# A hybrid decoder step on one Trainium2 core: token shift, decays, rates and key norms computed inside the projection stage instead of in a stage of their own

## The reference

```python
proj = x @ w_in
pr = proj[..., :RWKV_COLS]
shifted = jnp.concatenate([prev, pr[:, :-1]], axis=1)
mixed = pr + prm['tshift_mu'][i] * (shifted - pr)
...
w_log = -jax.nn.softplus(-(w0 + jnp.tanh(wd) @ w_w2)) - 0.5
decay = jnp.exp(-jnp.exp(w_log))
a = jax.nn.sigmoid(a0 + ad @ w_a2)
g = jax.nn.sigmoid(gd) @ w_g2
kk = heads(k * k_k)
kk = kk / jnp.maximum(jnp.linalg.norm(kk, axis=-1, keepdims=True), 1e-12)
k = k * (1.0 + (a - 1.0) * k_a)
y, S = wkv7_scan(r, decay, k, v, -kk, kk * a, S0)
```

## Time and profile before

| | |
|---|---|
| median of 3 runs | 1966.42 us (1962.9 to 1966.55) |
| the profiled execution | 1965.85 us, span 1963.7 us |
| PE / DVE / ACT / POOL busy | 1602.3 / 709.9 / 347.3 / 230.4 us |
| mean granted clock of TensorE | 0.873 of 2.4 GHz |
| transposes of x | 0 to 30 us |
| `project`, products | 30 to 313 us |
| `attend`, `attend_samples` | 313 to 426, 426 to 466 us |
| `shift_mix` | 466 to 574 us |
| `rwkv_sample` | 574 to 619 us |
| `rwkv_chunks`, `rwkv_norm` | 619 to 884, 884 to 960 us |
| `mix_out` and all after it | 960 to 1964 us |

### The profile page before, as it was taken

How to read it: one execution, slowest core, us unless ns; L and a number is a source line. 1 busy time by engine, 2 the same in 40 slices (tenths; PEclk the granted TensorE clock), 3 DMA queues, 4 the chain that set the end, 5 groups by cost and what they waited for, 6 DMA issues and landing times. The chain is left out here.

```text
span 1963.7 us, 29748 instructions
## 1 busy us (share of the span) xinstructions
PE 1602.3 (82%) x11876; PEld 1020.5 (52%) x11877; DVE 709.9 (36%) x1129; ACT 347.3 (18%) x753; POOL 230.4 (12%) x275
## 2 busy tenths in 40 slices
PE   6999996765522999985399949999959949999978
PEld 5666564544212888873145434444439834444433
DVE  1000000744965555546533341111159641111117
ACT  1000001541311322322000001111112201111111
POOL 3000000003002222303000001001040001100121
PEclk7999997885555999997699959999959959999989
DMA  7224201100011000000411267877750268887634
GB/s 230 99 93 121 107 1 33 46 23 5 0 27 23 4 4 4 4 6 5 118 44 33 94 232 272 294 278 275 243 193 1 88 211 282 288 289 240 212 141 168
DMA packets 134252, 237.09 MB, mean 121 GB/s; under 512 B 20434, under 2 KB 94147, under 8 KB 133866
## 3 DMA queue, kind: packets, MB, share of 16 engines
q1 hardware_dynamic: 110642, 150.94, 23.6%
q0 software_dynamic: 16880, 60.46, 8.4%
q10 hardware_dynamic: 6624, 24.12, 3.0%
HBM read 178.82 MB, written 58.21 MB: 121 GB/s over the span
## 5 line engine op out<-in xcount | busy, mean ns | idle before, releaser
L1985 PE MATMUL ex_pb<-ew_w_gate_up,ex_xT 128*128 x736 | 330.1, 602 | 5.9 <-DVE ex_xT L2025 2.3
L222 PE MATMUL pj_pb<-pj_xT,pj_w 128*128 128x344 f32 (+3 forms) x960 | 282.1, 457 | 0.4 <-ACT pj_xT L232 0.4
L222 PEld LDWEIGHTS pj_pb<-pj_xT,pj_w 128*128 128x128 f32 (+1 forms) x960 | 180.8, 188 | 101.2 <-issue 1.7
L1985 PEld LDWEIGHTS ex_pb<-ew_w_gate_up,ex_xT 128*128 128x128 f32 x736 | 137.9, 192 | 165.3 <-issue 164.4
L1968 PE MATMUL ex_pb<-ew_w_down,ex_hiddenT 128*128 x368 | 165.7, 593 | 3.4 <-ACT ex_hiddenT L2050 3.4
L2174 DVE TENSOR_TENSOR ex_hidden<-ex_hidden,ex_pb 128x256 f32<-128x256 f32 x46 | 19.4, 421 | 324.6 <-ACT ex_hidden L2045 324.6
L1968 PEld LDWEIGHTS ex_pb<-ew_w_down,ex_hiddenT 128*128 128x128 f32 x368 | 66.3, 190 | 69.9 <-issue 69.9
L1932 POOL COPY ex_tokens_now<-ex_token_of_slot 128x1 uint32 (+1 forms) x48 | 9.5, 199 | 745.5 <-PE ex_pb L1957 399.7
L1741 PE MATMUL mo_pb<-mo_w,projected 128*128 128x512 f32 (+1 forms) x144 | 65.8, 611 | 21.3 <-DMA mo_w<-in_w_out 21.3
L2169 DVE COPY ex_y_rows<-ex_pb 128x512 f32<-128x512 f32 x46 | 31.8, 692 | 134.5 <-PE ex_pb L1968 134.5
L238 DVE COPY projected<-pj_pb 128x344 f32<-128x344 f32 (+3 forms) x21 | 10.9, 519 | 187.9 <-PE pj_pb L222 187.9
(11 more groups left out here) (422 smaller groups left out, 2429.5 us busy)
## 6 DMA issues: line engine op xcount, KB each, us to landing
ew_w_gate_up<-in_w_ex_gate SPq DMA_DIRECT2D x32, 1024.0 KB
ew_w_gate_up<-in_w_ex_up SPq DMA_DIRECT2D x32, 1024.0 KB
ew_w_down<-in_w_ex_down SPq DMA_DIRECT2D x32, 1024.0 KB
scratch_slots_out<-ex_y_rows ACTq DMA_DIRECT2D x46, 512.0 KB
scratch_slots_out<-pj_zero POOLq DMA_DIRECT2D x4, 4096.0 KB
scratch_x_stored<-x_rows SPq DMA_DIRECT2D x16, 512.0 KB
pj_w<-in_w_in SPq DMA_DIRECT2D x3, 2048.0 KB, 18.6
pj_xt<-in_x_prompt SPq DMA_DIRECT2D x8, 512.0 KB
```

Of the source, the lines that this page charges most:

```text
L222: last = nc.tensor.matmul(pb[0:mrows, 4 + at % 4, 0:tn], w[:, s % NW, k, c0:c0 + mrows], xT[:, k, t0:t0 + tn], start=(k == 0), stop=(k == ...
L1985: last = mm(pb[:, 2 + u, :], xT[:, u, k, :], w[:, k, :], start=(k == 0), stop=(k == KD - 1))
```

## The change

`shift_mix` is gone. Its work is done in `project`, on products while they come:

- The order of the tiles is now 12, 13 (the inputs of decay, rate and gate), then the keys 4 to 7, then 0 to 3, 8 to 11, and 14 to 19 as before. Weight slabs have 256 columns at most, the first one 192.
- `xT` has a column of zeros ahead, and each product covers one token more on the left (348, 348 and 347 columns in place of 352, 344 and 344), so a product holds each token and the one before it. ACT scales the tokens' own part by 1 - mu out of PSUM; DVE adds mu times the token before, out of the same bank. Only tiles 14 to 19 are still copied in turn.
- TensorE gets 36 small products: after each key tile three for the decay and three for the rate, and after the next two tiles the sums of squares for the key norms, six in each. They use the other four banks of PSUM.
- ACT takes them with sigmoid or square root; DVE does the scan after each key tile, and from the eighth tile on the reciprocals and the products for the keys, in turn.
- The decay sums are kept as plain sums of sigmoids, with one zero ahead of each chunk of 64: the same buffer, read one column earlier, gives the sums before a token. The multiplication by -exp(-0.5) is the scale of the exponentials. In `rwkv_chunks` two exponentials for each tile take the place of three, the second over 130 columns a row.
- `attention_out` is gone: the attention's result is written over the q columns of `projected_qkv`.

The diff, cut to its core:

```diff
-def project(nc, io, pr, pq, keep, const):
+def project(nc, io, pr, A, B, U, pq, vec, keep, const):
-    slabs = [(0, 512), (512, 512), (1024, 512), (NR, WL + AL + GL), (NR + WL + AL + GL, 512),
-             (NR + WL + AL + GL + 512, 256)]
+    slabs = [(NR, WL + AL + GL, ((0, WL + AL, 12), (WL + AL, GL, 13)))]
+    slabs += [(HW * j, HW, ((0, P, 2 * j), (P, P, 2 * j + 1))) for j in (2, 3, 0, 1, 4, 5)]
+    slabs += [(QC + HW * j, HW, ((0, P, 14 + 2 * j), (P, P, 15 + 2 * j))) for j in range(3)]
-    cols = [(0, 352), (352, 344), (696, 344)]
+    thirds = [(0, 347, 347, 348), (347, 347, 347, 348), (694, 330, 338, 347)]
+    cuts = [(0, 384), (384, 384), (768, 264)]
+    FIRST_A, FIRST_N = 2, 6
...
+            def small_products(lhs, rhs):
+                nonlocal small
+                for t0, tn in cuts:
+                    if small >= 4:
+                        pe.wait_ge(s_taken, small - 3)
+                    nc.tensor.matmul(pb[:, small % 4, 0:tn], lhs, rhs[:, t0:t0 + tn], start=True, stop=True).then_inc(s_small, 1)
+                    small += 1
...
+                    before = at - 4
+                    if before >= 3 * MIXED:
+                        pe.wait_ge(s_cp[before % 2], (before - 3 * MIXED) // 2 + 1)
+                    elif before >= 0:
+                        pe.wait_ge(s_mix, before + 1)
...
+                t = i - FIRST_A
+                if 0 <= t < 4:
+                    if t == 0:
+                        pe.wait_ge(s_in, 32)
+                        pe.wait_ge(s_lora, 1)
+                    small_products(w2[:, P * t:P * t + P], pr[0:WL, 12, :])
+                    small_products(a2[:, P * t:P * t + P], pr[0:WL + AL, 12, :])
+                if i in (FIRST_N, FIRST_N + 1):
+                    for t in range(2):
+                        key_norms(2 * (i - FIRST_N) + t)
...
+                    act.wait_ge(s_mm, at + 1)
+                    nc.scalar.activation(pr[0:mrows, tile, t0:t0 + n], product(at)[:, 1:1 + n], ACT.Identity,
+                                         scale=omu[0:mrows, tile:tile + 1]).then_inc(s_now, 1)
...
+            def keys(t):
+                k = pr[:, 4 + t, :]
+                link(stt(out=A[:, t, :], in0=k, scalar=nkk[:, t:t + 1], in1=A[:, t, :], op0=ALU.mult, op1=ALU.mult))
+                link(nc.vector.tensor_scalar(tmp[:, :], B[:, t, :], -1.0, vec["k_a"][:, t:t + 1], ALU.add, ALU.mult))
+                link(stt(out=k, in0=tmp[:, :], scalar=1.0, in1=k, op0=ALU.add, op1=ALU.mult))
+                stt(out=B[:, t, :], in0=A[:, t, :], scalar=-1.0, in1=B[:, t, :], op0=ALU.mult, op1=ALU.mult)
...
+                    last = stt(out=out[:, 0:n_prompt], in0=product(at)[:, 0:n_prompt], scalar=mu, in1=out[:, 0:n_prompt],
+                               op0=ALU.mult, op1=ALU.add)
...
+                t, part = divmod(i - FIRST_N - 1, 2)
+                if 0 <= t < 4:
+                    if i == FIRST_N + 2:
+                        dve.wait_ge(s_slots, 16 * n_zeros)
+                    (inverse_norm, keys)[part](t)
...
-def shift_mix(nc, io, pr, mx, cumx, vec, const):
...
 (rwkv_chunks)
-                nc.scalar.activation(inv[:, :, :], pr[:, 8:12, c], ACT.Exp, scale=-1.0).then_inc(q["ex"], 1)
-                nc.scalar.activation(cumx[:, :, c], cumx[:, :, c], ACT.Exp)
+                nc.scalar.activation(inv[:, :, :].rearrange("p t (h s) -> p t h s", h=2), decays(n, 1), ACT.Exp,
+                                     scale=DECAY).then_inc(q["ex"], 1)
-                nc.scalar.activation(pr[:, 8:12, c], pr[:, 8:12, c], ACT.Exp).then_inc(q["ex"], 1)
+                both = U_[:, :, 2 * (CH + 1) * n:2 * (CH + 1) * (n + 1)]
+                nc.scalar.activation(both, both, ACT.Exp, scale=-DECAY).then_inc(q["ex"], 1)
```

More of the change, by code:

```diff
@@ L43 @@
 TC = TT + NS
-PC = TC + 1
-S0C, V0C = T + 1, T + 1 + NS
+PC = TT + 1
+S0C = T + 1
 DA = 512
@@ L64 @@
 CH = 64
+SC0 = (T // CH) * (CH + 1)
+UW = SC0 + NS
+DECAY = math.exp(-0.5)
 TILES = NT + 1
@@ L159, in project @@
         s_mm = m.sem("product")
-        s_ev = [m.sem(f"evacuated{i}") for i in range(2)]
+        s_now = m.sem("own_part")
+        s_mix = m.sem("mixed")
+        s_cp = [m.sem(f"qkv_copied{i}") for i in range(2)]
+        s_lora = m.sem("tanh")
+        s_small = m.sem("small_product")
+        s_taken = m.sem("small_taken")
+        s_sq = m.sem("squares")
+        s_vec = m.sem("vectors")
+        s_chain = m.sem("chain")
         s_z = m.sem("zeroed")
@@ L166, in project, with product @@
         xp = io["x_prompt"][0]
-        n_out = len(tiles) * 3
+        n_zeros = (NBLK + 7) // 8
+        n_keep = 16 * len(keep)
+        def product(at):
+            return pb[0:tiles[at // 3][2], 4 + at % 4, :]
         @block.sync
@@ L194, in _ @@
                     load_slab(0)
-            for s in range(1, len(slabs)):
+            load_slab(1)
+            sp.wait_ge(s_z, 1)
+            sp.dma_start(w2[:, :], io["decay_w2"][0]).then_inc(s_in, 16)
+            sp.dma_start(a2[WL:WL + AL, :], io["iclr_a2"][0]).then_inc(s_in, 16)
+            for s in range(2, len(slabs)):
                 load_slab(s)
@@ L231, in evacuate @@
                 src = pb[:, 2 * par:2 * par + 2, :].rearrange("p b (k t) -> p (b k) t", k=4)[:, :, 0:n]
[L232 to L238, removed]
+                copy(xT[:, :, 1 + P * i:1 + P * i + n], src).then_inc(s_xT[par], 1)
@@ L780, in rwkv_sample @@
-def rwkv_sample(nc, io, pr, mx, const):
+def rwkv_sample(nc, io, pr, A, B, U, const):
     with Memory(nc, "rs") as m:
@@ L841, in _ @@
         def _(act):
-            nc.scalar.activation(decay[:, :, :], pr[:, 8:12, T:TT], ACT.Exp).then_inc(q["pre"], 1)
+            nc.scalar.activation(decay[:, :, :], U[:, :, SC0:UW], ACT.Exp, scale=-DECAY).then_inc(q["pre"], 1)
             for j in range(6):
@@ L951, in take_rows @@
                 nc.scalar.copy(tok[:, j, :], pb[:, 2 + j % 2, :]).then_inc(q["tc"], 1)
-            nc.scalar.activation(ends[:, :, :], pr[:, 8:12, CH - 1:T:CH], ACT.Exp).then_inc(q["ex"], 1)
+            nc.scalar.activation(ends[:, :, :], U_[:, :, CH:SC0:CH + 1], ACT.Exp, scale=-DECAY).then_inc(q["ex"], 1)
             exps(0)
@@ L1350, in square @@
                     act.wait_ge(q["done"], t - 1)
-                nc.scalar.activation(sq[:, t % 2, :], pr[:, t, 0:TT], ACT.Square).then_inc(q["sq"], 1)
+                nc.scalar.activation(sq[:, t % 2, :], ya[:, t, 0:TT], ACT.Square).then_inc(q["sq"], 1)
             square(0)
```

426 lines of the change are left out of this document (191 added, 235 removed).

## The result

The changed kernel takes 1873.38 us in the median (1871.33 to 1877.35), against 1966.28 for the kernel before on the same chip: a ratio of 0.9531, 95% interval 0.9515 to 0.9547, or 92.9 us less. The forecast was 1875.3. The profiled execution took 1871.33 us with a span of 1869.2, 94.5 less than before's 1963.7.

What follows compares the result with a forecast made beforehand. TensorE was taken to bound `project`, DVE `shift_mix`. Terms -108.0 + 20.6 + 0.8 + 1.0 - 4.0 - 1.3 - 0.2 = -91.1 us gave 1875.3 us, range 1867 to 1890.

Steps and rivals of the forecast that it cites:

- The stage removed: `shift_mix` goes whole, from its first load to the first of `rwkv_sample`, barrier included: -108.0 us.
- The step on prices: In `project`, twelve sets of small products at 0.832 ns for a column of a pass add 20.6 us on TensorE.
- The handovers: In `project`, small products wait no longer than a handover: 36 more semaphores, +1.0 us for all, ends 0 and 15.
- Hidden on DVE and ACT: In `project`, about 85 us of DVE work and ACT's work stay under TensorE's cover: 0 us.
- that is three products, 13.8 us: In `project`, TensorE writes three products before needing DVE's mix, so DVE's run with its queue, 9.0 us, stays hidden.
- one tile is the limit: Rival for tripled reciprocals in `project`: cover is 13.8 us, four places stall 8 to 9 us each, +35; no chance given.
- The start: Before the first product, a first weight slab of 0.8 MB in place of 2 MB brings x earlier: -4.0 us.
- The lower end of 0: At the start, slab rows of 768 bytes in place of 2048 may cost the whole gain: 0 us.
- The table load: The load ahead of `rwkv_sample`'s exponential moves into ACT's idle time in `attend`, without a drain counted: -1.3 us.
- `rwkv_chunks`: One ACT exponential of three goes; only the first tile gains: -0.2 us, with -0.5 and +2.5 as ends.
- Waits at the small products: Rival in `project`: TensorE waits at six places, or its clock drops after them; about +13 us, 1888 us; chance 0.15.
- The clock that falls for good: Rival in `project`: gaps drop TensorE to the lower clock through the mixed part; +215 us, 2090 us; chance 0.02.

Runs made afterwards that it cites:

- e2: The kernel before, with each of the four reciprocals of `shift_mix` done three times in a row; 2010.24 us, ratio 1.023.
- e3: The changed kernel with each of the four key norm reciprocals in `project` done three times in a row; 1881.67 us, ratio 0.9573.
- e4: The changed kernel with each of the four key norm reciprocals in `project` done five times in a row; 1945.47 us, ratio 0.988.
- e5: The changed kernel with each of the 36 small products computed twice into the same bank; 1898.46 us, ratio 0.9664.
- e7: The changed kernel with an added square root in `attend_samples`, putting the table load back at the head of `rwkv_sample`; 1877.9 us, ratio 0.9552.
- e8: The changed kernel with a third exponential for each tile back on ACT in `rwkv_chunks`, into an unused buffer; 1870.5 us, ratio 0.9505.
- e1: The kernel before, with the 192-column weight slab and its two tiles put first; 1964.28 us, ratio 0.9987.
- e6: The changed kernel with the key norms' products in the same tile as the squares they need, not later; 1884.76 us, ratio 0.9588.

## Why the prediction was right

**The stage removed**, -108.0, came as priced: the work exposed costs its full length (e2, +53.1 for 52.8); covered it costs nothing, up to a limit (e3, e4).

**The small products.** The step on prices held (+20.5 in e5 for 20.6). The handovers were mis-sized: 22.3 - 20.6 = 1.7 us for twelve sets, not 1.0. With +0.8 for the three more columns this makes 23.1. The trace has 21.6 because the kernel before spent its first 4.3 us of products at the lower clock, 2.1 us lost, and the change's profiled execution did not: 21.6 + 2.1 = 23.7. The 0.6 us between 23.1 and 23.7 are not placed. In e3, e5, e7 and e8 the changed code does start at the lower level, and in e7, otherwise the same up to there, the phase lasts 306.7.

**Hidden on DVE and ACT**: right, 86.3 us against 85. But the step "that is three products, 13.8 us" is wrong. e3 shows four, and a cover of 16.7 us for a run of DVE (20.2 at the first tile). The run of 7.4 is less than half of that. The error was on the safe side; it would have mis-sized a longer run, as the 35 us of e3's third branch ("one tile is the limit") against 7.9 of waits show.

**The start**: -3.6 for -4.0. Of it 3.1 us are the earlier arrival of x (21.96 for 25.10), and the rest is a faster transpose, since the clock rose under the last ones (3.97 us for 24 passes, 4.79 before), less a wait for the last copy that is 0.4 us longer. In e3 to e8, with the same start, it is 27.1 to 28.0 us, and 27.5 in e1, so the slab is worth 2.3 to 3.2 us there and the -3.6 is the lucky end. The lower end of 0 was too careful; the rows of 768 bytes cost nothing that shows.

**The table load**: mechanism right, -1.6 in the stage for -1.3, with the clock in between. The Trainium skill (ScalarE: Activation LUTs, What ACT_TABLE_LOAD costs) puts a drain of about 1.38 us behind a load. The trace disagrees a second time: in e7 the exponential starts 0.02 us after the load ends. Nor is there a drain ahead of a load: in the change's `project` the load at 56.52 starts 0.02 us after the ACT instruction before it ends, and the next starts 0.01 us after it.

**`rwkv_chunks`**: -0.2 was predicted, and e8 shows 0 for the exponential. The 0.20 us of the earlier trace rows is how long GpSimd stood idle after its own memset, and no more than that could be gained; in the change its first product starts 0.17 us earlier in the stage, right behind the memset. Its first two products, the first at the pitch of 65, then take 1.45 and 1.25 us in place of 1.30 and 1.17, which gives it back. The -1.4 of this stage and the -2.0 of `rwkv_norm` were not foreseen; all later stages were to keep their lengths within a microsecond. The first goes with the change (see e8), cause open. `rwkv_norm` lasts 73.9 to 74.0 us in some runs and 75.8 to 76.3 in the others: 75.9 before but 74.0 in e2, which has the same code there, and 74.0 in the change but 75.9 in e7. So its -2.0 is no work of the change.

**The sum.** By mechanisms the profiled execution has -108.0 - 3.6 + 23.7 - 1.6 + 0.5 (the stages around) = -89.0, where I had -91.1; the -2.1 of the clock at the start of the products, the -1.4 of `rwkv_chunks` and the -2.0 of `rwkv_norm` gave -5.5 on top. The median's 92.9 lies between. So it is in part luck that the forecast is within 1.9 us of the median: added work mis-sized on the low side, and gains that the sum did not have, against each other.

**The rivals.** Waits at the small products: none on record in the change, but e6 shows how near they are, for one other placing. The clock that falls for good: not in the change, 1.00 over 305 us. The Trainium skill (TensorE: Matmul & The Clock Gate, A second HAM failure mode: psum-queue depth-cycling) reports a kernel whose clock swings because it goes round its PSUM banks with short idle times between groups of matmuls. Here four banks go round for the products and four for the small ones, but TensorE is idle for only 1.5 of 305 us and the granted clock shows no fall; so the change gave that rule hardly any idle time to work on, and does not test it. Falls do come with waits of 2 us and more (two of three of 2.0 us in e6, both of 3.78 in e3, all four in e4), and cost 1.5 to 2.9 us beside the wait itself.

## What to carry to other kernels

Work on an engine that idles beside a saturated TensorE is free only while its longest unbroken run stays below the products that TensorE may write ahead, and that limit is worth computing exactly. Here it was the number of banks in the ring, four, times a product, 4.6 us, less the mixes and the handover at its ends. Put a small dependent product a tile later than its operand is ready; the norms' products, put at once, added half of what all the small products together cost (11.8 of 22.3 us). When two executions differ by 1 to 2 us in a stage that the change does not touch, compare the granted clock at that stage's start, and the same stage in every other trace at hand, before looking for a cause.

## What was not expected of the hardware

- The clock fell without idle time: in e5 behind 3.65 us of matmuls of 32 rows, with TensorE busy throughout, in two of four like places, for 3.4 us each. In the change, with half as long a stretch of them, it did not.
- After a wait of 3.78 us the clock fell only when work had begun again: the 3.8 us of the wait itself have a granted 1.00, the 4.0 us behind them 0.57 (e3).
- It rose during transposes alone: 24 passes of them from 21.96 us, 0.50 from 22 to 24 us and 1.00 from 25 on, in the changed kernel.
- The late part of layer 1 lasts either 502 to 504 us or 509 to 512, whichever kernel runs. These 8 us are the largest difference between the profiled executions outside the stages that a run changes, and they are why stage lengths, not totals, carry the conclusions above. Its cause is open.
